# Moving a group's maxima and exponents to the third cache page, its weighing to the fourth, and the reload of its slots behind it

## The chip, the cores and the metric

One NeuronCore of one Trainium2 chip. The metric is the device time of one execution in microseconds (us), the median of several runs.

## The reference

One step of a hybrid decoder layer in float32, for 256 prompt tokens and 8 sampled tokens (one for each of 8 sequences). The part that matters is the attention of the 8 sampled tokens over a paged cache of 2048 past positions each, 16 pages of 128 positions:

```python
def page_block(phys):
    kn, kr, v = mla_keys(cache_l[phys], w_uk, w_uv, k_norm_nope)
    return partial_softmax(mla_scores(qn, qr, kn, kr), v)

def partial_softmax(s, v):
    m = jnp.max(s, axis=-1)
    p = jnp.exp(s - m[..., None])
    acc = jnp.einsum('bhqk,bkhd->bhqd', p.astype(v.dtype), v).astype(jnp.float32)
    return m, jnp.sum(p, axis=-1), acc
```

A key is the page's latent row times `w_uk`, divided by its root mean square per head; the partial results of the pages are merged with weights exp(m - max m). Beside it the layer has a gated DeltaNet branch (with a triangular inverse for each pair of heads), a prompt attention, gates, two output products and a squared-ReLU MLP.

## The kernel before, in words

Every engine has its own hand-written instruction stream, and semaphores tie them together. After a front part (projections, 0 to about 100 us) comes the **cache loop**: 128 iterations `n`, one for each page of the cache (8 sequences x 16 pages), from 101.7 to about 1140 us; then the gates (`z_unit`), the output products and the MLP. Four pages make a group: `g = n // 4`, `t = n % 4`, 32 groups, four groups to a sequence. Below, "iteration" is one `n`; t=0 is the group's first page, t=2 its third, t=3 its fourth.

In each iteration:
- SP (the queue of DMAs) issues `turn(n + 2)` (L522), a DMA transpose of the page's 16-bit planes. At certain steps it loads the pages of a whole group into the ring of 12 slots `clat`/`crope`: `page()` (L513 to L517), a read of the page table and two DMAs for each page. Before it overwrites slots it waits for `pv_used`, the weighing of the group that was in them. SP counts half iterations `i` (0 to 255, `i // 2 = n`); it also loads the weights and states of the side work.
- ScalarE: `turned_page(n + 1)` copies the transposed page into `cTr` (L834) and rounds it to `cTh` (L837). `squares` (L846) takes the sums of squares of the keys, once for each half of them. `exps` (L865, L866) takes exponents of a group's scores.
- VectorE: `split_lo(n + 1)` makes `cTl` (L1233), `split_planes(n + 3)` makes `planes` (L1228). For a group: `score_parts` (L1237), `scaled` (L1243, L1245), `maxima` (L1251 to L1260), `probabilities` (L1264), `accumulate` (L1268 to L1275, into `lacc`), and `latent_sum` once a sequence.
- GpSimd: `group` (L700 to L703): a power of the mean squares, then a small operation `gate`, then a maximum over all partitions, `smax`.
- TensorE: `keys(n, 0)` and `keys(n, 1)`, two halves of 12 matmuls of 512 columns each (L1991 to L1993). Between them it does the group's small work: `score_columns` (L2021) ahead of t=0, `weigh` (L2031) ahead of t=1, `rope_columns` (L2002) ahead of t=2, `query_products` (L2012, L2015) ahead of t=3. `weigh` multiplies the exponents `pst` with the raw latents in the ring and raises `pv_used`.

All engines also do **side work** in `beside(2n)` (start of an iteration) and `beside(2n + 1)` (its middle, between the key halves): the prompt attention, and from iteration 17 on the DeltaNet of four pairs of heads. In it, products need weights `bwl` that VectorE has split (L1286 for L2084 to L2086), rows are spread with `spread_row` (L2058, L2059) once VectorE has made them with `newton` (L1426 to L1430, L1134), and VectorE reads the spread rows (L1490). TensorE waits with `begin_a` until VectorE has read the bank used two steps ago. VectorE and ScalarE do an iteration's work in the order of the code: `beside(2n)`, `split_lo`, the group's steps, `beside(2n + 1)`, `split_planes`.

One iteration takes 5.7 us with nothing beside the keys, and up to 13 us with side work. In this profile iteration 17 starts at 246.93, 41 at 445.74, 44 at 474.77, 93 at 881.0, 100 at 938.27, 121 at 1096.77, 122 at 1102.49 and 123 at 1109.47 us.

Of the kernel before, what the change touches and what calls it, by code (L numbers as in the profile page):

```python
# [37 lines left out]
NT = NS * PAGES  # L38
NG = NT // 4
RING = 12  # L40
# [130 lines left out]
def pair_slot(i):  # L171

    k = i - B_START
    b, k = divmod(k, B_SLOTS)
    return (b, STEPS[k]) if 0 <= b < HP and STEPS[k] is not None else (None, None)
# [8 lines left out]
def build(nc, I, O):  # L184
    C_in, ctx = I["consts"], ExitStack()
    with ctx:
        sems = {}

        def S(name):
            if name not in sems:  # L190
                sems[name] = ctx.enter_context(nc.semaphore(name))
            return sems[name]
# [266 lines left out]
        def sum_bank(gg):  # L459

            return ps[:, 3 if gg < NG - 2 else 4, :]
# [19 lines left out]
        def _(sp):  # L481
# [31 lines left out]
            def page(u, n):  # L513
                pg = sp.value_load(ptab[0:1, bass.ds(n, 1)] if not isinstance(n, int) else ptab[0:1, n:n + 1], min_val=0, max_val=I["cache_mla"].shape[1] - 1)
                rows_ = I["cache_mla"][0][bass.ds(pg, 1), :, :].rearrange("o p n -> p (o n)")
                sp.dma_start(clat[:, u, :], rows_[:, 0:LAT]).then_inc(S(f"page_landed{u}"), 16)
                sp.dma_start(crope[:, u, :], rows_[:, LAT:LW]).then_inc(S(f"page_landed{u}"), 16)  # L517

            def turn(n):
                sp.wait_ge(S("planes_ready"), n - 1)  # L520
                wait(sp, "ct_raw", n - 1)
                sp.dma_start(turned[:, n % 2].bitcast(U16).rearrange("p (x n) -> p x n", n=P), planes[:].bitcast(U16), transpose=True).then_inc(S("tr_landed"), 16)  # L522
# [45 lines left out]
            def z_load(i):  # L568
                if i < 2:
                    sp.wait_ge(S("gdn_out"), 16 * 9 * HP)  # L570
                    sp.wait_ge(S("a_read"), len(SIDE_A))
                else:
                    sp.wait_ge(S("w_hi"), NP + i - 1)
                    sp.wait_ge(S("w_lo"), NP + i - 1)
                sp.dma_start(wraw2[:, i % 2], win[:, 4 * (i % 2):4 * (i % 2) + 4, z_columns(i):z_columns(i) + 512]).then_inc(S(f"z_landed{i % 2}"), 16)

            def front_loads(i):
                if i == 2:
                    sp.wait_ge(S("qrs_ready"), 1)
                    sp.dma_start(qr64[0:64, :, :], qr[64:128, :, TP:T]).then_inc(S("qr64_landed"), 16)  # L580
                    sp.dma_start(qr64[64:128, :, :], qr[0:64, :, TP:T]).then_inc(S("qr64_landed"), 16)
                if i == F_NOPE + 6:
                    sp.wait_ge(S("b_read"), b_count("row5"))
                    for t in range(2):
                        sp.dma_start(O["rows_prompt"][0, 0, P * t:P * t + P, :], ltok[t][:]).then_inc(S("rows_out"), 16)
                    sp.dma_start(O["rows_sample"][0, :, 0, :], ltok[2][0:NS, :]).then_inc(S("rows_out"), 16)
                if i == F_END - 1:
                    sp.wait_ge(S("rows_out"), 48)
                    sp.wait_ge(S("a_read"), a_count(f"pv{H - 1}"))
                    for jj in range(2):  # L590
                        pair_weights(jj)
                    pair_rows_in(0)
                if i == B_START - 1:
                    pair_weights(2)

            sp.dma_start(O["conv_sample"][0, :, 0:CONVW - 2, :], I["state_conv"][0, :, 1:CONVW - 1, :]).then_inc(S("conv_shift"), 16)
            for i in range(2 * NT):
                n = (i - 3) // 2 + RING - 8
                if i % 8 == 3 and i >= 16 and n < NT:
                    sp.wait_ge(S("pv_used"), i // 8 - 1)  # L600
                    for m in range(n, n + 4):
                        page(m % RING, m)
                if i % 2 == 0 and i // 2 + 2 < NT:
                    turn(i // 2 + 2)
                front_loads(i)
                b, k = pair_slot(i)
                if b is not None:
                    pair_loads(b, k)
                if i == B_START + HP * B_SLOTS + 1:
                    z_load(0)  # L610
                    z_load(1)
                if i == 2 * NT - 3:
                    z_load(2)
                    z_load(3)
# [94 lines left out]
        def _(act):  # L709
# [139 lines left out]
            def turned_rope(gg):  # L849
                act.wait_ge(S("rope_done"), gg + 1)  # L850
                wait(act, "qk_done", gg)
                nc.scalar.activation(rpT[:], ps[:, B_SCORE, 0:2 * P], ACT.Copy).then_inc(S("rope_ready"), 1)
# [142 lines left out]
            for n in range(NT):  # L995
                g, t = n // 4, n % 4
                if n + 1 < NT:
                    turned_page(n + 1)
                if t == 2:
                    turned_rope(g)  # L1000
                if t == 3:
                    score_rows(g)
                beside(2 * n)
                squares(n, 0)
                if t == 3 and g >= 1:
                    exps(g - 1)
                beside(2 * n + 1)
                squares(n, 1)
# [73 lines left out]
        def _(v):  # L1082
# [553 lines left out]
            for n in range(NT):  # L1636
                g, t = n // 4, n % 4
                beside(2 * n)
                if n + 1 < NT:
                    split_lo(n + 1)  # L1640
                if t == 0 and g >= 1:
                    score_parts(g - 1)
                if t == 1 and g >= 1:
                    scaled(g - 1)
                if t == 1 and g >= 2:
                    probabilities(g - 2)
                    accumulate(g - 2)
                if t == 3 and g >= 1:
                    maxima(g - 1)
                if n == NT - 1:  # L1650
                    score_parts(g)
                beside(2 * n + 1)
                if n + 3 < NT:
                    split_planes(n + 3)
                if t == 2 and g >= 2 and g % 4 == 1:
                    latent_sum(g // 4 - 1)
                if t == 3:
                    v.wait_ge(S("ksq_ready"), 2 * n + 2)
                    V.tensor_scalar(kss[:, g % 2], kss[:, g % 2], 1.0 / 128, EPS, ALU.mult, ALU.add).then_inc(S("ms_ready"), 1)  # L1659
# [157 lines left out]
            for g in range(2):  # L1817
                for u in range(8):
                    n = 8 * g + u + 3
# [11 lines left out]
        def _(pe):  # L1831
# [106 lines left out]
            for c in range(KC):  # L1938
                i = mm(b[:, 0:T], wmisc[:, c, 0:128], xn[:, c, :], start=c == 0, stop=c == KC - 1)
            i.then_inc(S("side_done"), 1)  # L1940
            b = begin("decay_raw")
            for c in range(KC):
                i = mm(b[0:64, 0:T], wmisc[:, c, 128:192], xn[:, c, :], start=c == 0, stop=c == KC - 1)
# [16 lines left out]
            for p in range(4):  # L1960
                i = mm(rows_b[32 * p:32 * p + 8, 0:T], consts[:, C_ZP.start + 2:C_ZP.start + 10], sq[:, p, :], start=False, stop=False)
# [8 lines left out]
            for h in range(H):  # L1970
                if h >= 4:
                    pe.wait_ge(S("ukT_act" if h % 2 == 0 else "ukT_dve"), (h - 4) // 2 + 1)
                for c in range(4):
                    i = nc.tensor.transpose(ps[:, 4 + h % 4, 128 * c:128 * c + 128], ukf[c][:, 128 * h:128 * h + 128], ident)
# [49 lines left out]
            def weigh(gg):  # L2024
                pe.wait_ge(S("pst_ready"), gg + 1)
                if gg >= NG - 2:
                    pe.wait_ge(S("s_parts"), NG)
                wait(pe, "acc_done", gg)
                wait(pe, "accT_ready", gg // 4)
                for t in range(4):  # L2030
                    k = mm(sum_bank(gg)[32 * t:32 * t + 32], pst[:, gg % 2, t, :], clat[:, (4 * gg + t) % RING, :], start=True, stop=True)  # L2031
                k.then_inc(S("pv_used"), 1)

            def latent_columns(s_):
                pe.wait_ge(S("acc_done"), 4 * s_ + 4)
                for c in range(4):
                    k = nc.tensor.transpose(latent_bank(s_)[:, c, :], lacc[:, P * c:P * c + P], ident)
                k.then_inc(S("pvt_done"), 1)
# [275 lines left out]
            for n in range(NT):  # L2314
                g, t = n // 4, n % 4
                if t == 3:
                    query_products(g)
                if n == 0:
                    transposes(1)
                if t == 0 and g >= 1:  # L2320
                    score_columns(g - 1)
                if t == 1 and g >= 2:
                    weigh(g - 2)
                if t == 2:
                    rope_columns(g)
                beside(2 * n)
                keys(n, 0)
                if t == 2 and g >= 2 and g % 4 == 1:
                    latent_columns(g // 4 - 1)
                if n == NT - 1:  # L2330
                    score_columns(g)
                beside(2 * n + 1)
                keys(n, 1)
# [146 lines left out]
```

## Time and profile before

| what | value |
|---|---|
| median of 3 runs (lowest to highest) | 1484.63 us (1483.99 to 1484.95) |
| the profiled execution, own time | 1484.91 us |
| its span, first to last instruction | 1483.1 us |
| mean granted TensorE clock | 0.998 |
| TensorE busy (PE) | 1473.2 us, 99% |
| weight loads (PEld) | 1221.0 us, 82% |
| VectorE (DVE), ScalarE (ACT), GpSimd (POOL) busy | 813.6, 878.8, 216.0 us |
| chain that ended last | PE 97%, DVE 2%, ACT 1% |
| DMA | 173.92 MB, mean 117 GB/s |

All times are us. The chain of waits is followed back from the last instruction. PE is TensorE's matmuls, PEld its weight loads, SPq the queue of SP. L with a number is the line of the kernel. A matmul's end is modelled, so its start is the safer number.

### The profile page before, as it was taken

Reading aid. Unit: us, or ns where it says so; the run is one execution under the profiler, and the core shown is the slowest. Engines: PE = TensorE matmul, PEld = TensorE weight load, DVE = VectorE, ACT = ScalarE, POOL = GpSimd, SP = SyncE. Lnnn points to the kernel's source line nnn. Section 1 sums busy time; section 2 is a strip of 40 time slices with the busy share of each in tenths; the row PEclk is TensorE's granted clock in tenths of the full one; section 3 lists DMA queues with packets and bytes.
Section 4 is the critical chain, followed back from the end, with each engine's and each line's share of the span. In section 5 each row is a group of like instructions: output and inputs, shape, how many; then the busy total and the mean of one; then the engine's idle time right before and its main releaser. Section 6 shows DMA issues by size and latency. Waiting matters only on the chain.

```text
span 1483.1 us, 26962 instructions
## 1 busy us (share of the span) xinstructions
PE 1473.2 (99%) x9284; PEld 1221.0 (82%) x9284; DVE 813.6 (55%) x1596; ACT 878.8 (59%) x2836; POOL 216.0 (15%) x111
## 2 busy tenths in 40 slices
PE   9999999999999999999999999999999999999998
PEld 7877777877877778778777777788777999999998
DVE  5864445555445563555554555645423766787643
ACT  5545678686566675576855666765766353444432
POOL 3001111211121111111221111111313000000000
PEclk9999999999999999999999999999999999999999
DMA  9542315643245443255323464322654465555551
GB/s 286 169 116 36 78 31 129 153 96 63 61 98 128 119 91 71 61 128 135 83 61 68 102 153 73 68 62 64 169 100 128 151 222 196 171 171 171 190 178 58
DMA packets 263714, 173.92 MB, mean 117 GB/s; under 512 B 165464, under 2 KB 212088, under 8 KB 263448
## 3 DMA queue, kind: packets, MB, share of 16 engines
q1 hardware_dynamic: 263266, 171.94, 44.5%
q8 instruction: 72, 1.18, 0.3%
q14 instruction: 58, 0.48, 0.1%
q10 hardware_dynamic: 318, 0.33, 0.1%
HBM read 132.63 MB, written 6.74 MB: 94 GB/s over the span
## 4 chain that ended last, share of the span: by engine, by line
PE 97%; DVE 2%; ACT 1%; issue 0%; POOL 0%; DVEq 0%; ACTq 0%
PE ps L1991 17%; PE ps L1993 16%; PE ps L1992 16%; PE ps L2400 6%; PE ps L2401 6%; PE ps L2402 5%; PE ps L2031 2%; PE ps L2012 2%; PE ps L2084 2%; PE ps L2348 2%; PE ps L2349 2%; PE ps L2085 2%; PE ps L2086 2%; PE ps L2350 2%; PE ps L1869 2%; PE ps L2150 2%
## 5 line engine op out<-in xcount | busy, mean ns | idle before, releaser
L846 ACT ACTIVATE ksq<-ps 128x128 f32<-128x128 f32 x1024 | 268.1, 276 | 295.0 <-PE ps L1993 293.7
L1991 PE MATMUL ps<-ukh,cTh 128*128 128x512 f32 x1024 | 417.9, 408 | 0.3 <-DVE cTl L1233 0.3
L1993 PE MATMUL ps<-ukh,cTl 128*128 128x512 f32 x1024 | 401.7, 392 | 0.0
L1992 PE MATMUL ps<-ukl,cTh 128*128 128x512 f32 x1024 | 400.4, 391 | 0.0
L700 POOL TENSOR_TENSOR rk<-kss,mhalf 128x32 f32<-128x32 f32 x32 | 179.7, 5616 | 496.8 <-DVE kss L1659 496.8
L1991 PEld LDWEIGHTS ps<-ukh,cTh 128*128 128x128 f32 x1024 | 192.8, 188 | 53.8 <-issue 17.1
L1993 PEld LDWEIGHTS ps<-ukh,cTl 128*128 128x128 f32 x1024 | 192.3, 188 | 42.6
L1992 PEld LDWEIGHTS ps<-ukl,cTh 128*128 128x128 f32 x1024 | 193.2, 189 | 34.1
L846 ACT ACTIVATION_READ_ACCUMULATOR ksq<-ps 128x1 f32 x1024 | 212.2, 207 | 0.0
L834 ACT ACTIVATE cTr<-turned 128x1024 uint16<-128x1024 uint16 x126 | 173.9, 1380 | 10.9 <-PE ps L2015 6.7
L1035 ACT ACTIVATE wh<-wraw 128x2048 fp32r<-128x2048 f32 x44 | 84.3, 1916 | 131.7 <-PE ps L2402 127.2
L1233 DVE TENSOR_TENSOR cTl<-cTr,cTh 128x512 fp32r<-128x512 f32 x128 | 88.3, 690 | 125.4 <-ACT cTh L837 124.4
L1663 DVE TENSOR_TENSOR wl<-wraw,wh 128x2048 fp32r<-128x2048 f32 x44 | 100.8, 2291 | 70.1 <-ACT wh L1035 70.1
L1228 DVE COPY planes<-clat 128x1024 uint16<-128x1024 uint16 x126 | 86.4, 686 | 19.4 <-DMA turned<-planes 13.3
L2400 PE MATMUL ps<-Ah,wh 128*128 128x264 f32 x320 | 91.2, 285 | 0.0
L2401 PE MATMUL ps<-Al,wh 128*128 128x264 f32 x320 | 91.0, 284 | 0.0
L2402 PE MATMUL ps<-Ah,wl 128*128 128x264 f32 x320 | 90.7, 284 | 0.0
L837 ACT ACTIVATE cTh<-cTr 128x512 fp32r<-128x512 f32 x128 | 80.9, 632 | 4.1
L2400 PE MATMUL ps<-Hh,wh 128*128 128x264 f32 x256 | 72.8, 285 | 0.0
L2402 PE MATMUL ps<-Hh,wl 128*128 128x264 f32 x256 | 72.8, 284 | 0.0
L2401 PE MATMUL ps<-Hl,wh 128*128 128x264 f32 x256 | 72.7, 284 | 0.0
L2400 PEld LDWEIGHTS ps<-Ah,wh 128*128 128x128 f32 x320 | 60.3, 188 | 0.0
(501 smaller groups left out, 2692.4 us busy)
## 6 DMA issues: line engine op xcount, KB each, us to landing
clat<-cache_mla SPq DMA_DIRECT2D x128, 256.0 KB, 2.6
wraw<-w_in SPq DMA_DIRECT2D x16, 1024.0 KB, 5.1
wraw<-w_up SPq DMA_DIRECT2D x16, 1024.0 KB, 5.3
wraw<-w_down SPq DMA_DIRECT2D x16, 1024.0 KB, 5.0
braw<-w_in SPq DMA_DIRECT2D x24, 512.0 KB, 4.1
crope<-cache_mla SPq DMA_DIRECT2D x128, 32.0 KB, 2.4
sst<-state_gdn SPq DMA_DIRECT2D x32, 128.0 KB, 3.3
gdn_sample<-sst SPq DMA_DIRECT2D x32, 128.0 KB, 2.0
```

The costliest lines, as they stand in the source:

```text
L700: nc.gpsimd.tensor_tensor(rk[:, y], kss[:, y], mhalf[:], ALU.pow).then_inc(S("rk_ready"), 1)
L834: nc.scalar.activation(cTr[:, :, tokens(n)].bitcast(U16).rearrange("p c (t x) -> p x c t", x=2), turned[:, n % 2].bitcast(U16).rearrange(" ...
L846: i = nc.scalar.activation(ksq[:, P * h:P * h + P], ps[:, k % 3, P * h:P * h + P], ACT.Square, accum_out=kss[:, n // 4 % 2, n % 4, 4 * hal ...
L1228: V.tensor_copy(planes[:].bitcast(U16).rearrange("p (x l) -> p x l", x=2), clat[:, n % RING, :].bitcast(U16).rearrange("p (l x) -> p x l", ...
L1233: V.tensor_tensor(cTl[:, n % 2], cTr[:, :, tokens(n)], cTh[:, n % 2].bitcast(F32), ALU.subtract).then_inc(S("ct_lo"), 1)
L1663: V.tensor_tensor(wl2[:, ns % 2], wraw2[:, (ns - NM) % 4], wh2[:, ns % 2].bitcast(F32), ALU.subtract).then_inc(S("w_lo"), 1)
L1991: mm(out, cTh[:, n % 2, c], ukh[:, c, cols], start=c == 0, stop=False)
L1992: mm(out, cTh[:, n % 2, c], ukl[:, c, cols], start=False, stop=False)
L1993: i = mm(out, cTl[:, n % 2, c], ukh[:, c, cols], start=False, stop=c == 3)
L2400: mm(out, w_hi, mh[:, kc, :], start=first and kc == 0, stop=False)
L2401: mm(out, w_hi, ml[:, kc, :], start=False, stop=False)
L2402: k = mm(out, w_lo, mh[:, kc, :], start=False, stop=last and kc == 3)
```

## The change

Four steps of a group move; nothing is added or taken away. `maxima` and `exps` of group g-1 go from t=3 to t=2. `probabilities` and `accumulate` of group g-2 go from t=1 to t=0. `weigh` goes from the start of t=1 (of group g-2) to the middle of t=3 (of group g-1). The loads of a group's pages go from the second half of t=1 to the second half of t=3 two iterations earlier, and wait for the weighing in that same iteration.

```diff
@@ SP
             for i in range(2 * NT):
-                n = (i - 3) // 2 + RING - 8
-                if i % 8 == 3 and i >= 16 and n < NT:
-                    sp.wait_ge(S("pv_used"), i // 8 - 1)
+                n = (i + 1) // 2 + RING - 8
+                if i % 8 == 7 and i >= 15 and n < NT:
+                    sp.wait_ge(S("pv_used"), i // 8)
                     for m in range(n, n + 4):
                         page(m % RING, m)
                 if i % 2 == 0 and i // 2 + 2 < NT:
@@ ScalarE
                 beside(2 * n)
                 squares(n, 0)
-                if t == 3 and g >= 1:
+                if t == 2 and g >= 1:
                     exps(g - 1)
                 beside(2 * n + 1)
                 squares(n, 1)
@@ VectorE
                 if t == 1 and g >= 1:
                     scaled(g - 1)
-                if t == 1 and g >= 2:
+                if t == 0 and g >= 2:
                     probabilities(g - 2)
                     accumulate(g - 2)
-                if t == 3 and g >= 1:
+                if t == 2 and g >= 1:
                     maxima(g - 1)
@@ TensorE
                 if t == 0 and g >= 1:
                     score_columns(g - 1)
-                if t == 1 and g >= 2:
-                    weigh(g - 2)
                 if t == 2:
                     rope_columns(g)
                 beside(2 * n)
                 keys(n, 0)
                 if t == 2 and g >= 2 and g % 4 == 1:
                     latent_columns(g // 4 - 1)
+                if t == 3 and 1 <= g < NG - 1:
+                    weigh(g - 1)
                 if n == NT - 1:
                     score_columns(g)
                 beside(2 * n + 1)
                 keys(n, 1)
```

## Rows read from the trace of the kernel before

**Rows 1.** The page, part 1: busy us (share of the span) x instructions.
```profile
PE 1473.2 (99%) x9284; PEld 1221.0 (82%) x9284; DVE 813.6 (55%) x1596; ACT 878.8 (59%) x2836; POOL 216.0 (15%) x111
```

**Rows 2.** Waits of TensorE: waiter <- waited for: us in total, times, longest.
```profile
PE ps L2084 <- DVE bwl L1286: 0.4, 1, 0.4
...
PE ps L1991 <- DVE cTl L1233: 0.3, 1, 0.3
```

**Rows 3.** Timeline of TensorE around the start of iteration 121: start, us, engine, line.
```profile
1095.23 0.39 PE L1992 MATMUL ps<-ukl,cTh 128*128 128x512 f32 x1
1095.46 0.39 PE L1993 MATMUL ps<-ukh,cTl 128*128 128x512 f32 x1
1095.78 1.07 PE L2031 MATMUL ps<-clat,pst 128*32 128x512 f32 x8
1096.77 0.50 PE L1991 MATMUL ps<-ukh,cTh 128*128 128x512 f32 x1
```

**Rows 4.** Waits of all engines, the one for pages just landed.
```profile
DVE planes L1228 <- DMA crope<-cache_mla: 5.0, 3, 3.3
```

**Rows 5.** Timeline of VectorE and TensorE in iteration 44.
```profile
478.40 1.21 DVE L1286 TENSOR_TENSOR bwl<-braw,bwh 128x1024 fp32r<-128x1024 f32 x1
...
480.32 1.06 PE L2031 MATMUL ps<-clat,pst 128*32 128x512 f32 x8
...
481.32 0.39 PE L2084 MATMUL ps<-Ah,bwh 128*128 128x264 f32 x1
```

**Rows 6.** Timeline of VectorE in iteration 93, from probabilities to the split of `bwl`.
```profile
884.63 0.20 DVE L1264 TENSOR_REDUCE lall<-pst 128x8 f32<-128x32 f32 x1
...
885.92 1.23 DVE L1286 TENSOR_TENSOR bwl<-braw,bwh 128x1024 fp32r<-128x1024 f32 x1
```

**Rows 7.** Timeline of VectorE in iterations 121 and 122.
```profile
1099.81 0.19 DVE L1245 TENSOR_TENSOR ssc<-sparts,ssc 128x32 f32<-128x32 f32 x1
...
1100.04 0.68 DVE L1275 COPY lacc<-ps 128x512 f32<-128x512 f32 x1
...
1105.64 0.69 DVE L1233 TENSOR_TENSOR cTl<-cTr,cTh 128x512 fp32r<-128x512 f32 x1 [4.18 <-ACT cTh L837]
```

**Rows 8.** Timeline of VectorE and TensorE in iterations 40 and 41.
```profile
443.77 1.79 DVE L1426 RECIPROCAL lr<-lr 64x264 f32<-64x264 f32 x1 [0.71 <-ACT lr L972]
...
447.62 0.42 DVE L1134 TENSOR_TENSOR lrl<-lr,lrh 64x264 fp32r<-64x264 f32 x1
...
448.69 0.39 PE L2058 MATMUL ps<-lrh,idr 64*128 64x264 f32 x1
```

**Rows 9.** Timeline of VectorE and TensorE in iteration 100.
```profile
943.76 0.77 DVE L1490 TENSOR_TENSOR qkv<-qkv,ps 128x264 f32<-128x264 f32 x2
...
944.42 1.07 PE L2031 MATMUL ps<-clat,pst 128*32 128x512 f32 x8
```

**Rows 10.** Timeline of VectorE and TensorE at the start of iteration 17.
```profile
246.11 0.69 DVE L1233 TENSOR_TENSOR cTl<-cTr,cTh 128x512 fp32r<-128x512 f32 x1 [1.73 <-ACT cTh L837]
...
246.93 0.50 PE L1991 MATMUL ps<-ukh,cTh 128*128 128x512 f32 x1
```

**Rows 11.** Timeline of ScalarE in iteration 15.
```profile
239.81 1.28 ACT L865 ACT_TABLE_LOAD   x1
```

**Rows 12.** Timeline of GpSimd beside iterations 121 and 122.
```profile
1100.08 0.18 POOL L702 TENSOR_TENSOR gate<-mhalf 1x1 f32<-1x1 f32 x1 [3.17 <-DVE ssc L1245]
1106.70 0.45 POOL L703 PARTITION_ALL_REDUCE smax<-ssc  x1 [6.44 <-issue]
```

**Rows 13.** Timeline of TensorE, the first key matmul of iteration 123.
```profile
1109.47 0.50 PE L1991 MATMUL ps<-ukh,cTh 128*128 128x512 f32 x1
```

**Rows 14.** Timeline of SP's queue, the block of page loads in iteration 121.
```profile
1097.63 0.35 SPq L516 DMA_DIRECT2D clat<-cache_mla  x1
...
1103.42 5.54 SPq L522 DMA_TRANSPOSE turned<-planes  x2
```

**Rows 15.** The tile `turned`: the landing of its DMA transposes.
```profile
DMA to landing us min/median/max: 3.0/3.1/5.3
```

## The prediction

> **What bounds the kernel now.** I read the page's busy times, then the list of TensorE's waits, then the timeline of single stretches of the cache loop. The reader is to see three things. TensorE is busy for 99% of the span [rows 1]. In the whole loop it waits for another engine twice: 0.3 us for `cTl` in the very first iteration, which the change does not touch, and 0.4 us for `bwl` in iteration 93 [rows 2]. And the spaces between its matmuls are its own work: key matmuls start 0.23 us apart, and where a weighing stands between two of them the distance is 1.31 us (1095.46 to 1096.77), whoever else is early or late [rows 3]. So the loop is TensorE's own queue, and a change that alters only the order of work can gain that one wait of 0.4. What it can lose is any cover that is gone.
>
> The change aims at waits off TensorE: VectorE's 5.0 us at `split_planes` for pages just landed [rows 4]. TensorE is covered there, so I count that gain as nothing.
>
> The Trainium skill, "Perfetto Trace Analysis", section "Identifying the Most-Contended Engine", says that matmul busy time is a bad measure of headroom. By that rule the 99% proves little, and bubbles could be hidden inside it; it is a rival below. The even 0.23 us starts of rows 3 speak against it here.
>
> **The change part by part.** Sizes are us; times are made against the profiled execution (1484.91, span 1483.1, 1.8 around it), which stands 0.28 above the median of 1484.63.
>
> *Weighing*, from ahead of the keys of t=1 to between the key halves of t=3, which is two iterations sooner for its group. It costs TensorE 1.31 - 0.23 = 1.08 [rows 3]; 30 are moved and 30 issued, so the sum is 0. What changes is where they cover: everything that TensorE needs at the start of a t=1 iteration is now needed about 1.0 sooner (weighing starts at 480.32 and the product behind it at 481.32 [rows 5]). At t=3 it is the other way round, 1.0 of new cover.
>
> *Probabilities and accumulate*, from t=1 to t=0 on VectorE, one iteration sooner. From the first of them to the next operation is 885.92 - 884.63 = 1.29 [rows 6]; for every fourth group a copy, 0.68 alone [rows 7]. They now stand in front of VectorE's answer to `beside(2n+1)` of t=0. So at one border, t=0 to t=1, VectorE is up to 1.29 later and TensorE 1.0 earlier: 2.3 of slack is used. I looked at all t=0 iterations; in five the slack is smaller.
> - Iteration 44 (and 92, whose pattern is the same to 0.01): `bwl` ends at 478.40 + 1.21 = 479.61; with 1.2 in front, 480.8; TensorE will want it at 480.32 [rows 5]. Stall 0.5, twice: 1.0. Bounds for the pair: 0, if something else moves TensorE back, to 2 x 1.0 = 2.0, if VectorE is late by as much again.
> - Iterations 40 and 41: the copy form fits in the 0.71 that VectorE idles ahead of the reciprocal, so the Newton chain still ends at 447.62 + 0.42 = 448.04. TensorE's `ob` row now starts at 448.69, after the move at 447.55 (1.0 and 0.14 less, the key half being shorter without a break ahead of it) [rows 8]. Stall 0.5, bounds 0 to 1.1.
> - Iteration 100: the `lb` products are read at 943.76 and over 0.77; TensorE will want the bank at 944.42 [rows 9]. With 1.2 in front it stalls 1.0; but the exponents' table load no longer stands in iteration 99, which frees ScalarE and brings `cTl` about 0.9 sooner. I take 0.3, bounds 0 to 1.1.
> - Iteration 17: `cTl` was ready at 246.11 + 0.69 = 246.80 for the keys at 246.93 [rows 10], a slack of 0.1, and these keys now come 1.0 sooner. But in iteration 15 ScalarE loads a table of 1.28 for the exponents [rows 11], because a logarithm's table stood in its place; at t=2 of the same group they come ahead of that logarithm, and the load and the exponents (0.4) leave the queue in front of this `cTl`. 1.6 sooner against 1.0: stall 0, bounds 0 to 0.9.
>
> Together +1.8. One old wait goes: at iteration 93 `bwl` no longer has accumulate in front [rows 6], -0.4. **Sum: +1.8 - 0.4 = +1.4.**
>
> *Maxima and exponents* from t=3 to t=2. `scaled` ends at 1099.81 + 0.19 = 1100.00; GpSimd's gate starts at 1100.08, its reduction at 1106.70 and lasts 0.45: 7.15 from scores to maxima [rows 7, 12]. VectorE would reach the maxima at 1105.64 + 0.69 = 1106.33 [rows 7], so it now waits: 0.8 here, and about 1.2 more since the t=0 half before it starts 1.08 + 0.14 later. Behind it queue the rest of VectorE's iteration (side work, `split_planes` and so the next transpose), and on ScalarE the exponents, the second squares and the next `turned_page`. TensorE at the end of t=2 has the query products first and then the next keys; `cTl` for those was done at 1106.33 and is used at 1109.47, 3.1 later [rows 7, 13]. With 2.0 of wait and 0.9 for the maxima, the following `cTl` is about 1.2 late against a slack of some 3. Cost 0, bounds 0 to 2.0 for each short iteration, of which there are some nine.
>
> *Page loads*, from the second half of t=1 to that of t=3, two iterations sooner for their group. A block of four occupies SP from 1097.63 to the transpose at 1103.42, 5.8, whatever it waits for [rows 14]. It now waits for a weighing that ends some 3.9 into t=3, so the transpose behind it is issued at about +10.5 and lands at +13.6 by the median landing of 3.1, at +15.8 by the longest of 5.3 [rows 15]. ScalarE wants it at +12.8. Late by 0.8 to 3.0, then 2.8 for copy, cast and split; TensorE needs the result at +18.1. 13.6 + 2.8 = 16.4 has 1.7 left; 15.8 + 2.8 = 18.6 is 0.5 short. Cost 0; bounds 0 to 0.5 in each of the seven blocks with short iterations behind them, 3.5. The longer waits on SP for `pv_used` also hold back pair weights, but these are asked for two products ahead. No DMA is added: 29 blocks before, 29 after. DMA traffic around the z loads (t=0 of iteration 116) is the one new neighbour; I give it 0 to 2.
>
> On the median this makes 1484.63 + 1.4 = 1486.0.
>
> **Rivals.**
> 1. *VectorE's answers at t=0 (slower).* Place: iterations 17, 41, 44, 92 and 100, with 76 and 69 as the next in line. Price: the upper bounds above, 2.0 + 1.1 + 1.1 + 0.9 = 5.1, less 0.4: +4.7, 1489.3. It decides once the stalls sum to over 3.4. For: `bwl` already reached TensorE 0.4 late with accumulate in front of it [rows 2, 6]. Against: in the other t=0 iterations I find 0.8 and more left.
> 2. *The transpose behind the page block (slower).* 3.5 + 2 + 1.4 gives +6.9, 1491.5. It decides if the landings behind a block are nearer 5.3 than 3.1; the median over all 126 is 3.1 and blocks stand in front of 29 of them today, so I hold it unlikely.
> 3. *The changed order is never felt.* All stalls are inside slack I have read too small; the old wait goes: -0.4, 1484.2. For: slacks were read to 0.1 with modelled matmul ends.
> 4. *Hidden bubbles (faster).* If TensorE's 99% held bubbles that the earlier page loads remove, each of 29 blocks might give back 0.2, -5.8, 1478.8. Against: rows 3. The skill's rule named above is its only ground.
>
> **How the numbers follow.** 0.2% is 3.0 us, about what a measurement of this kernel can tell from no change. Forecast (+1.4, from 0 to +2.9): 0.65. Rival 3: 0.14. Rival 1: 0.13. Rival 2: 0.05. Rival 4: 0.03. Faster by over 0.2%: 0.03; within: 0.65 + 0.14 = 0.79; slower: 0.18. The range takes in rival 3 (1484.2, less 0.6 for the spread of runs, which were 1483.99 to 1484.95) and reaches to 1488.8, nearly rival 1. Left out are rivals 2 and 4 and the far half of rival 1, some 0.15.
>
> **What would show it.** In TensorE's waits of the changed kernel: `bwl` in the neighbourhood of iterations 44 and 92, 0.5 each, and the one of 93 gone; L2058 waiting for VectorE in iterations 41 and 100; no wait for `cTl` in iteration 17. The distance over a weighing is again 1.31, now between the halves of t=3, and the t=1 border of a short iteration is 0.23. On VectorE, L1251 waits for GpSimd in the short groups, up to 2 each, 10 to 15 in all, where it was 1.8; on SP the wait for the weighing grows; VectorE's 5.0 for landed pages is gone; one ScalarE table load fewer. I am wrong if TensorE waits for `cTl` in t=2 iterations (rival 2), if its waits sum to over 4 (rival 1), or if key matmuls stand closer than 0.23.

## The result, and the profile after

| | before | changed |
|---|---|---|
| median (lowest to highest), 7 runs each | 1484.37 us (1483.70 to 1484.95) | 1489.88 us (1489.15 to 1490.66) |
| ratio, 95% interval | | 1.0039 (1.0029 to 1.0048) |
| span of the profiled execution | 1483.1 us | 1488.8 us |
| first key matmul of iteration 0 to the first of the second key half of iteration 127 ("the loop" below) | 101.66 to 1137.93 = 1036.27 us | 101.68 to 1143.67 = 1041.99 us |

The change costs 5.5 us by the medians; between the two profiled executions the cache loop alone is 5.72 longer. I had forecast +1.4 with a range up to 1488.8. The measured time lies above it.

The page after, part 1, busy us (share of the span) x instructions. Compare it with [rows 1]: the share of TensorE is again 99%, and that of its weight loads again 82%. Neither would have told anything of the 5.5 us.

```profile
PE 1474.9 (99%) x9284; PEld 1219.4 (82%) x9284; DVE 815.3 (55%) x1596; ACT 878.9 (59%) x2835; POOL 222.2 (15%) x111
```

The waits of TensorE in the changed kernel, those in the cache loop (us in total, times, longest). Compare them with [rows 2]: before, there was one wait for `bwl` of 0.4, and the same 0.3 for `cTl` in iteration 0.

```profile
PE ps L2058 <- DVE lrl L1134: 1.8, 2, 1.1
...
PE ps L2084 <- DVE bwl L1286: 1.5, 3, 0.6
...
PE ps L2289 <- ACT pT L916: 0.5, 1, 0.5
PE ps L2058 <- DVE qkv L1490: 0.4, 1, 0.4
...
PE ps L1991 <- DVE cTl L1233: 0.3, 1, 0.3
```

Without that 0.3 these are 4.2 us of waits in seven places, against 0.4. Four of the places I had forecast: `bwl` in iterations 44 and 92, and iterations 41 and 100. Iterations 13 and 90 I had not, and 69 only as "next in line" in rival 1. The sum is over the 4 that the prediction had named as its sign of being wrong. Waits of other engines in the changed kernel; the wait for landed pages of [rows 4] is gone, and three others have grown (before: 13.3 for the transposes, 1.8 at L1251, 15.1 for the weighing on SP's queue):

```profile
DVE planes L1228 <- DMA turned<-planes: 36.1, 25, 3.6
...
DVE mall L1251 <- POOL smax L703: 14.2, 14, 4.4
```

```profile
SPq L514 <- PE ps L2031: 142.5, 28, 8.6
```

**A ledger of distances.** A wait in the list is shorter than the time that it costs, and the list has none of the costs that are not waits. Here is the timeline of TensorE in iteration 44 of the changed kernel:

```profile
482.97 0.39 PE L1993 MATMUL ps<-ukh,cTl 128*128 128x512 f32 x1
483.94 0.39 PE L2084 MATMUL ps<-Ah,bwh 128*128 128x264 f32 x1 [0.59 <-DVE bwl L1286]
```

The list says 0.59. From the last key matmul ahead of this break to the first behind it the changed kernel takes 3.98, and 3.14 where nothing stalls there (e5 below), so 0.84 are lost. The rows show where the rest is: without the stall the product starts 0.23 behind the last key matmul (in e5 at 482.46 behind 482.23), here 0.97, which is 0.74; and the matmul behind it follows after 0.23 (484.17) where in e5 it is 0.12, another 0.11. So I compare, for each of the 256 key halves, the distance from the last key matmul of one to the first of the next, between two traces. Most of them agree to 0.01, so what is left is the change. For the changed kernel against before (us):

| where | sum |
|---|---|
| middle of t=3: 30 weighings added | +33.79 |
| border t=0 to t=1: 30 weighings gone, with the stalls of 44, 92 and 100 in it | -31.00 |
| middle of t=1: iteration 13 +0.72, 41 +0.72, 69 +0.61, the rest 0.13 | +2.18 |
| border t=1 to t=2: the old wait of iteration 93 -0.62, 45 -0.17, 65 +0.15 | -0.64 |
| middle of t=2: iteration 90 | +1.16 |
| the key halves themselves | +0.20 |

Together 5.7. The experiments take it apart.

### The profile page after: what moved, and what is told of

It reads as the page before. It is cut to its first block, busy times and chain, and to the rows that moved or that the text cites. A ratio compares the mean times of both kernels' runs of the same rounds, so it can differ in the third digit from the quotient of the medians.

```text
span 1488.8 us, 26959 instructions
## 1 busy us (share of the span) xinstructions
PE 1474.9 (99%) x9284; PEld 1219.4 (82%) x9284; DVE 815.3 (55%) x1596; ACT 878.9 (59%) x2835; POOL 222.2 (15%) x111
## 3 DMA queue, kind: packets, MB, share of 16 engines
q8 instruction: 72, 1.18, 0.3%
## 4 chain that ended last, share of the span: by engine, by line
PE 92%; DVE 3%; ACT 1%; SPq 1%; DMA 1%; issue 1%; POOL 0%; DVEq 0%; ACTq 0%
PE ps L1991 15%; PE ps L1993 14%; PE ps L1992 14%; PE ps L2400 6%; PE ps L2401 5%; PE ps L2402 5%; PE ps L2031 2%; PE ps L2012 2%; PE ps L2348 2%; PE ps L2349 2%; PE ps L2084 2%; PE ps L2350 2%; PE ps L2150 2%; PE ps L1869 2%; PE ps L2085 1%; PE ps L2086 1%
## 5 line engine op out<-in xcount | busy, mean ns | idle before, releaser
L1228 DVE COPY planes<-clat 128x1024 uint16<-128x1024 uint16 x126 | 86.6, 687 | 36.2 <-DMA turned<-planes 36.1
```

The source lines that it names most:

```text
L1228: V.tensor_copy(planes[:].bitcast(U16).rearrange("p (x l) -> p x l", x=2), clat[:, n % RING, :].bitcast(U16).rearrange("p (l x) -> p x l", ...
```

## The experiments

All times below are against the runs of the kernel before in the same job (medians 1484.27 to 1484.37). "Loop" is the distance defined above, from one profiled execution of each kernel.

| run | median | against before | loop against before |
|---|---|---|---|
| changed | 1489.88 | +5.5 | +5.72 |
| e1 maxima and exps only | 1484.37 | +0.1 | +0.06 |
| e2 = e1 + weighing moved | 1487.30 | +3.0 | +3.02 |
| e3 = e2 + page loads moved | 1487.79 | +3.5 | +3.94 |
| e4 = e2 + accumulate moved | 1488.80 | +4.5 | +4.45 |
| e5 changed, accumulate late in t=0 | 1487.34 | +3.1 | +3.21 |
| e6 changed, pages behind the transpose | 1490.16 | +5.9 | +6.15 |
| e7 = e5 + e6 | 1488.59 | +4.3 | +5.26 |
| e8 = e2, three weighings put back | 1485.30 | +1.0 | +0.99 |
| e9 before, accumulate late in t=1 | 1483.90 | -0.4 | -0.81 |
| e10 = e9 + e1 | 1483.56 | -0.8 | -0.80 |

The two columns need not agree to the tenth. In the profiled executions of e3, e4, e6 and e7 the granted clock of the first 100 us is 1.00 and the loop starts at 100.2 to 100.4; in before and changed it is 0.97 and the loop starts at 101.7. In the loop the clock is 1.00 in all twelve. The intervals of the medians are some 0.2% wide (3 us), so parts of 1.5 and less rest on the traces, one execution each.

**e1: maxima and exponents alone.**

```diff
-                if t == 3 and g >= 1:
+                if t == 2 and g >= 1:
                     exps(g - 1)
...
-                if t == 3 and g >= 1:
+                if t == 2 and g >= 1:
                     maxima(g - 1)
```

> The kernel before with one part alone: maxima and exps of group g-1 at t=2; weighing, accumulate and page loads stay. Theory 'lost cover' (what costs is the weighing that no longer stands between t=0 and t=1): -0.5 to +0.4 against before, TensorE waits 0 to 1 time in the loop beside the old ones of iterations 0 and 93. Rival 'maxima wait for GpSimd': +1 or more, with TensorE waits behind a VectorE that stood at L1251.

Median +0.1, ratio 1.0 (0.9991 to 1.0009). No distance in the loop moved by more than 0.02. The waits of VectorE for GpSimd and of TensorE in the loop:

```profile
DVE mall L1251 <- POOL smax L703: 8.6, 8, 2.1
```

```profile
PE ps L2084 <- DVE bwl L1286: 0.4, 1, 0.4
...
PE ps L1991 <- DVE cTl L1233: 0.3, 1, 0.3
```

The wait that I had worked out at up to 2.0 is there (longest 2.1), and it never reaches TensorE. By itself this part of the change is free.

**e2: the weighing as well.** The changed kernel with accumulate and page loads back in their old places, so against e1 only the weighing moves:

```diff
-                if t == 1 and g >= 2:
-                    weigh(g - 2)
...
+                if t == 3 and 1 <= g < NG - 1:
+                    weigh(g - 1)
```

> The changed kernel with accumulate back at t=1 and the page loads back in the second half of t=1; so against e1 only the weighing moves. Theory 'lost cover': +4.5 against before: +0.95 for the shape of the breaks around the weighings, 0.7 each in iterations 13 and 41, 1.0 in 90, and the old wait of 0.6 (start to start) in iteration 93 grows by 1.1 since its chain too began ahead of the weighing; iterations 44, 69, 92 and 100 without a stall. Rival 'VectorE is late by accumulate' (my prediction's main term): +0.5 at most, since accumulate is not in front of t=0 answers.

+3.0 rather than +4.5: the stalls of 13 (+0.75), 41 (+0.63) and 90 (+0.90) are there and nothing else stalls; the old wait of iteration 93 did not grow (0.62 start to start before, 0.63 here), because its chain starts at `qkv`, which waits for the last product of the pair (881.20 before), and these products stand behind the place of the weighing (877.00). The rest, 3.02 - 2.28 = 0.74, is the weighings themselves: +33.79 in the middle of t=3, -33.32 at the border of t=1, +0.24 in the key halves. VectorE has the same work in the same places as in e1, so none of this 3.0 comes from the move of accumulate. It is more than half of the loss. The prediction had 0.5 of it, the stall of iteration 41.

**e8: three of 30 weighings back.** The direct test of cover:

```diff
+                if t == 1 and g in (3, 10, 22):
+                    weigh(g - 2)
...
-                if t == 3 and 1 <= g < NG - 1:
+                if t == 3 and 1 <= g < NG - 1 and g + 1 not in (3, 10, 22):
                     weigh(g - 1)
```

> e2 with three of its 30 weighings (groups 1, 8 and 20) put back at the start of t=1, in iterations 13, 41 and 89. Theory 'lost cover': just these three covered the stalls of 13, 41 and 90, which vanish: -2.3 against e2, +0.7 against before, the 0.7 being the shape of the breaks of 27 weighings. Rival 'the weighing in the middle of t=3 delays what follows it': -0.2 against e2 (three of 30), the stalls stay.

Three weighings at the start of iterations 13, 41 and 89 take away 2.0 us, and every one of the three stalls: in the middle of t=1, at the border t=1 to t=2 and in the middle of t=2 no distance differs from before by more than 0.02. The stalls were 2.3; the other 0.3 is in the breaks and key halves, which cost 1.0 here and 0.7 in e2. The timelines of iterations 88 to 90 show how. In the kernel before, ScalarE, VectorE and TensorE (three answers, one chain):

```profile
844.44 0.28 ACT L846 ACTIVATE ksq<-ps 128x128 f32<-128x128 f32 x1 [2.39 <-PE ps L1993]
...
847.52 1.28 ACT L972 ACT_TABLE_LOAD   x1
...
853.19 0.43 DVE L1134 TENSOR_TENSOR lrl<-lr,lrh 64x264 fp32r<-64x264 f32 x1
...
853.97 0.39 PE L2058 MATMUL ps<-lrh,idr 64*128 64x264 f32 x1
```

The chain is started by the key half (88, 1), ahead of the weighing: squares, copy and cast of the page, a table load, a root, then seven operations of VectorE. It takes 853.62 - 844.44 = 9.18. TensorE takes 853.97 - 844.44 = 9.53 over the same stretch, the weighing in it. Slack 0.35. With the weighing and its break elsewhere (1.2 less), TensorE is there after 8.3 and waits 0.9. In the changed kernel:

```profile
849.05 0.28 ACT L846 ACTIVATE ksq<-ps 128x128 f32<-128x128 f32 x1 [2.39 <-PE ps L1993]
...
858.08 0.42 DVE L1134 TENSOR_TENSOR lrl<-lr,lrh 64x264 fp32r<-64x264 f32 x1
...
858.56 0.38 PE L2058 MATMUL ps<-lrh,idr 64*128 64x264 f32 x1 [1.11 <-DVE lrl L1134]
```

And in e8, with the weighing of group 20 back:

```profile
844.39 1.06 PE L2031 MATMUL ps<-clat,pst 128*32 128x512 f32 x8
...
854.05 0.39 PE L2058 MATMUL ps<-lrh,idr 64*128 64x264 f32 x1
```

The stall of 90 lies one and a half iterations behind the place that the weighing left. That is why looking at the t=0 to t=1 border could not find it.

**e3: the page loads as well.** e2 with the page loads of the changed kernel (second half of t=3).

> The changed kernel with probabilities and accumulate back at t=1, all else as changed. Lost cover: about the same as the changed kernel, +5.3 against before: stalls of 44, 92 and 100 (2.0) gone, but iteration 93 now 1.7; iteration 69 stays at 0.6. Rival 'accumulate in front of the answers at t=0 is the cost': +1.5 to +2.5.

+3.5 by the medians, +3.94 in the loop; expected 5.3. The result lies between the theory and its rival. Two parts were too high: iteration 93 (0.64, not 1.7) and iteration 69 (0.17, not 0.6). Against e2 iteration 90 grows from 0.90 to 1.55 and 69 gets its 0.17; VectorE's wait for the transposes is the longest of all kernels:

```profile
DVE planes L1228 <- DMA turned<-planes: 52.8, 28, 4.9
```

The eleven runs of this kernel lie between 1487.45 and 1490.23, a wider spread than that of any other kernel here, and the profiled one (1487.64) is near the lower end. So its stalls may differ from one execution to the next.

**e4: accumulate instead of the page loads.** e2 with probabilities and accumulate at t=0, which is the changed kernel with the page loads put back.

> The changed kernel with the page loads back in the second half of t=1, all else as changed. Theory: the page block ahead of the transpose costs only iteration 69 (0.6) and 0.2 of iteration 90: +4.7 against before, VectorE's waits for the transpose (L1228 <- turned) back from 36 to about 13. Rival 'transposes behind the page block are most of it': +2 or less.

+4.5 (expected 4.7). Accumulate at t=0 costs 4.45 - 3.02 = 1.4: the border t=0 to t=1 saves 31.03 where it saved 33.32, so 2.3 of stalls in iterations 44, 92 and 100, 0.08 more in 41, less the old waits of 93 (0.62) and 45 (0.17). The page loads on top cost 5.72 - 4.45 = 1.3: iteration 69 (0.61), 0.33 more in 90, 0.15 in 65, 0.14 in 53. The 0.61 of iteration 69 needs both moves: in e3, with the page loads alone, it is 0.17, and in e4 nothing. In the same way the 2.3 of iterations 44, 92 and 100 need accumulate at t=0 and the weighing gone from the border. By [rows 5] and the `bwl` end worked out from them (480.8), `bwl` would still come ahead of the product at 481.32 if the weighing stood there; that is an estimate, no run has accumulate at t=0 with the weighing in its old place. Not all of VectorE's waits went back to what they were before: 17.5 for transposes and 18.1 for pages just landed, where it was 13.3 and 5.0.

The stall of 69 in the changed kernel, on SP's queue and on VectorE:

```profile
675.57 0.33 SPq L517 DMA_DIRECT2D crope<-cache_mla  x1
675.95 4.02 SPq L553 DMA_DIRECT2D sst<-state_gdn  x8
680.07 1.45 SPq L522 DMA_TRANSPOSE turned<-planes  x1
```

```profile
685.10 0.69 DVE L1228 COPY planes<-clat 128x1024 uint16<-128x1024 uint16 x1 [1.24 <-DMA turned<-planes]
685.71 1.22 DVE L1286 TENSOR_TENSOR bwl<-braw,bwh 128x1024 fp32r<-128x1024 f32 x1
```

SP waits 1.5 for the weighing of that iteration; then the block of pages (from 670.20) and eight state loads stand in front of the transpose. VectorE waits 1.24 at `split_planes`, `bwl` queues behind it, and TensorE stands 0.35 (0.5 start to start) for `bwl`. ScalarE's use of the transposed page, which I had examined, is not what stalls TensorE here.

**e5: accumulate behind the middle of t=0.**

```diff
                 if t == 0 and g >= 2:
-                    probabilities(g - 2)
-                    accumulate(g - 2)
...
                 beside(2 * n + 1)
+                if t == 0 and g >= 2:
+                    probabilities(g - 2)
+                    accumulate(g - 2)
```

> The changed kernel with probabilities and accumulate still in the iteration t=0, but behind VectorE's answers of its middle (after beside(2n+1)) instead of ahead of them. Theory 'place in VectorE's queue': the stalls of iterations 44, 92 and 100 (0.8, 0.8, 0.5 start to start) go and the old one of 93 stays away; 13, 41, 69 and 90 stay: -2.0 against the changed kernel, +3.5 against before. Rival 'these three too are lost cover of the weighing': no change against the changed kernel, +5.5.

2.5 faster than the changed kernel (expected 2.0); 44, 92, 100 and 93 without a stall. 13, 41 and 90 stay, 69 grows from 0.61 to 0.84. It holds e2's stalls without the old wait of 93, plus one of the page loads.

**e6: the pages behind the transpose.**

```diff
-                n = (i + 1) // 2 + RING - 8
-                if i % 8 == 7 and i >= 15 and n < NT:
-                    sp.wait_ge(S("pv_used"), i // 8)
-                    for m in range(n, n + 4):
-                        page(m % RING, m)
                 if i % 2 == 0 and i // 2 + 2 < NT:
                     turn(i // 2 + 2)
+                n = i // 2 + RING - 8
+                if i % 8 == 0 and i >= 16 and n < NT:
+                    sp.wait_ge(S("pv_used"), i // 8 - 1)
+                    for m in range(n, n + 4):
+                        page(m % RING, m)
```

> The changed kernel with the block of page loads one half iteration later on SP, directly behind the transpose in its queue. Theory 'the block stands in front of the transpose': stall of iteration 69 gone, that of 90 smaller by 0.3, VectorE's waits for the transposes (L1228 <- turned) from 36 to under 20; about -1.2 against the changed kernel, +4.4 against before. Rival 'the earlier DMA traffic itself slows the transposes': no change, +5.5.

A miss: slower than the changed kernel, +5.9. The stall of 69 is gone and that of 90 is down to 0.84, as expected, but two new ones stand in iterations 66 (0.78) and 118 (0.76). VectorE waits 23.9 for the transposes, not under 20. The two new waits of TensorE:

```profile
PE ps L2012 <- issue: 0.7, 1, 0.7
PE ps L2084 <- DVE oT L1607: 0.6, 1, 0.6
```

The block is now in front of the next transpose. In iteration 65, SP and then VectorE:

```profile
647.59 0.33 SPq L517 DMA_DIRECT2D crope<-cache_mla  x1
647.97 4.18 SPq L564 DMA_DIRECT2D gdn_sample<-sst  x8
652.26 1.27 SPq L522 DMA_TRANSPOSE turned<-planes  x1
```

```profile
655.46 0.69 DVE L1228 COPY planes<-clat 128x1024 uint16<-128x1024 uint16 x1 [3.16 <-DMA turned<-planes]
```

Both theories have a part in it: a queue of one engine only passes the block on to another transpose, and in iteration 118, behind the loads for z (L575 at 1074.34), ScalarE waited 3.30 for a transpose (`cTr` at 1085.09) whose landing is the longest of this kernel, 9.7 us, against 5.3 in [rows 15] (in e7, with the pages in the same place, the longest is 9.2). Whether traffic or the order of the DMAs did that is not told apart. SP and ScalarE there:

```profile
1075.38 15.62 SPq L522 DMA_TRANSPOSE turned<-planes  x3
```

```profile
1085.09 1.37 ACT L834 ACTIVATE cTr<-turned 128x1024 uint16<-128x1024 uint16 x1 [3.30 <-DMA turned<-planes]
```

**e7: both remedies.**

> Both of the two before in one kernel. What is left is the moved weighing (3.0 in e2) less the old wait of iteration 93 (0.6): +2.4 against before; stalls in 13, 41 and 90 only. Rival 'the parts interact and one remedy gives nothing beside the other': +3.5 or more.

+4.3 by the medians, expected 2.4: the rival holds. 13, 41 and 90 stay, 44, 92 and 100 are gone, and 66 (0.93), 69 (0.51), 102 (0.98), 118 (0.21) and 127 (0.47) stall. The remedy for accumulate works here as in e5, that for the pages does not. Its loop is +5.26 in the profiled execution, more than the median of its runs shows (1488.59; they lie between 1487.80 and 1489.06). The profiled one is among the slowest, 1488.95, although its first part is 1.2 shorter than in the profile of before. Stalls that hang on the landing of a DMA may differ between executions; no second profile of a kernel is there to show it.

**e9 and e10: a version that beats both?** The one old wait of the loop is accumulate in front of `bwl` in iteration 93 [rows 6].

```diff
-                if t == 1 and g >= 2:
-                    probabilities(g - 2)
-                    accumulate(g - 2)
...
                 beside(2 * n + 1)
+                if t == 1 and g >= 2:
+                    probabilities(g - 2)
+                    accumulate(g - 2)
```

> The kernel before with one edit: probabilities and accumulate stay in t=1 but go behind VectorE's answers of the middle. Theory 'place in VectorE's queue': the wait of iteration 93 for bwl (0.6 start to start) goes and nothing new comes, -0.6 against before (1483.7 where before is 1484.3). Rival 'another answer is then late': 0 or slower.

> e9 and e1 together: accumulate behind the middle of t=1, maxima and exps at t=2. e1 moved no distance in the cache loop by more than 0.02, so the same as e9, -0.6. Rival 'their waits add up on VectorE': a stall behind L1251 or L1275, 0 or slower.

The loop of both is 0.8 shorter, from exactly two distances: iteration 93 (-0.62) and iteration 45 (-0.17). No wait for `bwl` is left. VectorE in iteration 93 of e9, `bwl` now ahead of accumulate:

```profile
884.07 1.22 DVE L1286 TENSOR_TENSOR bwl<-braw,bwh 128x1024 fp32r<-128x1024 f32 x1
885.21 0.20 DVE L1264 TENSOR_REDUCE lall<-pst 128x8 f32<-128x32 f32 x1
```

Medians 1483.90 and 1483.56 against 1484.34, ratios 0.9997 (0.9988 to 1.0006) and 0.9995 (0.9986 to 1.0004). The traces show a gain of 0.8; the timing alone can't tell it from none.

## Why the prediction was wrong

The forecast was +1.4; the loop lost 5.7. The difference of 4.3 has four parts: two stalls that I did not see, iterations 13 and 90 (1.65 in e2), and 0.1 more in 41; the moved weighings themselves (0.7, forecast 0); accumulate (+1.4, forecast 1.0 + 0.3 - 0.4 = 0.9); and the page loads (+1.3, forecast 0). The first is the step that failed. Weighings and accumulate are terms of the sum with a wrong size, and the page loads took a path that I had not looked at (point 5).

1. *"a change that alters only the order of work can gain that one wait of 0.4. What it can lose is any cover that is gone"*: right in kind. e9 takes just that wait (0.62 from start to start, and 0.17 in iteration 45 that no list shows), and the change lost more than it took. Rival 4, bubbles that better feeding would fill, gave nothing: VectorE's 5.0 for landed pages went away and no distance became shorter by it. By the Trainium skill ("Perfetto Trace Analysis", section "Identifying the Most-Contended Engine") matmul busy time is a bad measure of headroom; the traces agree in this, that it stood at 99% of the span in both kernels while seven stalls cost 5.5 us.
2. *"30 are moved and 30 issued, so the sum is 0"*: mis-sized. The moved weighings cost +0.7 (e2; in e8, where nothing stalls, +1.0 for 27 of them). What a weighing costs depends on its neighbours. At the short pages it is 1.09 in the break and 0.14 in the key half behind it, where it stood as where it stands. But in iteration 72 it takes away only 1.74 - 0.75 = 0.99, because the product beside it starts 0.32 behind the last key matmul without the weighing too. In iteration 71 the product beside it had followed at 0.24; there the weighing adds 1.18. TensorE in the changed kernel, iterations 71 and 72:

```profile
706.28 0.39 PE L1993 MATMUL ps<-ukh,cTl 128*128 128x512 f32 x1
706.60 1.06 PE L2031 MATMUL ps<-clat,pst 128*32 128x512 f32 x8
707.60 0.39 PE L2084 MATMUL ps<-Ah,bwh 128*128 128x264 f32 x1
```

```profile
719.92 0.39 PE L1993 MATMUL ps<-ukh,cTl 128*128 128x512 f32 x1
720.24 0.39 PE L2058 MATMUL ps<-rwh,idr 64*128 64x264 f32 x1
```

3. *"So at one border, t=0 to t=1"* and *"I looked at all t=0 iterations"*: this is the step that failed. Taking 1.2 us of TensorE's own work out of a stretch shortens the cover of every chain that starts ahead of it and ends behind it, wherever that end is. I looked for answers near the border. One that TensorE needs in the middle of t=1 (iteration 13, `pT`, 0.75) and one in the middle of t=2 (iteration 90, `lrl`, 0.90) start before the border too. Iteration 41 I had, and by this very reasoning: accumulate fits into idle time, TensorE comes sooner, stall 0.5; e2 has 0.63 there with accumulate in its old place. The three are 2.3 of e2's 3.0, and e8 shows it with three weighings. For iteration 13, here are ScalarE before, from the key half ahead of the weighing (217.68) to `pT`, and TensorE in the changed kernel:

```profile
217.78 0.28 ACT L846 ACTIVATE ksq<-ps 128x128 f32<-128x128 f32 x1 [0.42 <-PE ps L1993]
...
221.43 0.47 ACT L916 ACTIVATE pT<-ps 128x384 f32<-128x384 f32 x1
```

```profile
223.34 0.52 PE L2289 MATMUL ps<-consts_sb,pr 128*128 128x128 f32 x3 [0.54 <-ACT pT L916]
```

4. *Accumulate ahead of the answers at t=0*: the mechanism right, the size low. Predicted 0.5 + 0.5 + 0.3 for iterations 44, 92 and 100 less 0.4 for 93; measured 0.84 + 0.85 + 0.64 = 2.3 less 0.8. The end of `bwl` was read nearly rightly: `bwl` was forecast to end at 480.8 and does so at 483.89, in a loop that is 2.96 later by then, which is 480.93. The need was read 0.1 late: I took the start of the weighing (480.32) for it, but with the weighing gone the product can follow the last key matmul after 0.23 rather than 0.32. A further 0.1 each are the end of `bwl` and the slower second matmul behind a stall.
5. *Page loads "Cost 0"*, with bounds up to 3.5: +1.3 in the changed kernel, +0.9 in e3. I asked only whether ScalarE gets the transposed page in time for TensorE's keys; `cTl` was never late. But VectorE waits for the same transpose at `split_planes`, 36.1 us in all, and what stands behind that in its order (`bwl` in iteration 69) is side work with less slack than the keys.
6. *Maxima "Cost 0"*: right (e1), and the sum of the waits too (14.2, forecast 10 to 15). But one of them, in iteration 66 of the changed kernel, is 4.4 where I had up to 2; why stays open. *Iteration 17*: right, no wait; one ScalarE instruction fewer, the table load.
7. *The chances*: rival 1, at 0.13, was nearest with +4.7, and its sign came true (waits over 4). That it was so near is luck in good part: with accumulate out of the way +3.1 remain (e5). Rival 2 had page loads as a cost, but through `cTl`, for which TensorE never waited in the loop after iteration 0. The t=1 border at the short pages is 0.23 as forecast.

```profile
1102.36 0.39 PE L1993 MATMUL ps<-ukh,cTl 128*128 128x512 f32 x1
1102.59 0.39 PE L1991 MATMUL ps<-ukh,cTh 128*128 128x512 f32 x1
```

The traces say more on the 0.32 and the 0.23. In that of before, every matmul of the form 128*128 that comes directly behind a key half starts 0.23 or 0.24 behind its last matmul (136 of them). Those of the forms 128*8 to 128*64, 64*128 and 24*128, the weighings (128*32) among them, all start 0.32 behind it (81); 128*11 and 96*128 (4 each) start at 0.23 and 0.24. This goes with the cost of a weighing: less next to a product of 64*128 (iteration 72) than next to one of 128*128 (iteration 71). That the form is the cause was not tried.

Open: how much of the late landings in e6 and e7 is traffic.

## What to carry to other kernels

When a block of the bottleneck engine's own work is moved, its length is taken from the slack of every chain that spans its old place. List the chains by where they start, and follow each to its end, which may lie one or two iterations on; the place itself shows only some of them. Where one engine is nearly always busy, compare distances from start to start between two traces, place by place: nearly all agree to 0.01 us, and the few that don't are the answer, while busy time says 99% in both.

## What the runs showed of the hardware that I had not expected

A stall of TensorE costs more than the wait that is listed: 0.59 listed and 0.84 lost in iteration 44, 0.35 and 0.61 in iteration 69, 0.65 and 0.72 in iteration 41. Eight weighing matmuls cost 1.18 us in one place and gave back 0.99 or 0.86 in another; behind a key matmul the form of the next one goes with a start after 0.23 or after 0.32. And a DMA transpose of the same size landed after 3.1 us in the median, and after 9.7 at the longest in e6.
